# Two steps moved out of a feed-forward's first stage, and two squares summed by TensorE: one edit to a two-network kernel on one core

## The reference, cut to what matters

```python
for l in range(2):
    h = h + 0.5 * swiglu(rmsnorm_2(h, ffn1_norm[l]), ...)      # ffn1_0, ffn1_1
    u = rmsnorm_2(h, mix_norm[l])
    if l == 0:
        h = h + pool_mixer(u, pool_w[0], pool_scale[0])        # the pooling
    else:
        h = h + mla_attention(u, ..., k_nope, k_rope, v, cos, sin)
    h = h + 0.5 * swiglu(rmsnorm_2(h, ffn2_norm[l]), ...)      # ffn2_0, ffn2_1
    if l == 0:                                                  # mla_shared_kv
        ckr = rmsnorm_2(h, kv_in_norm) @ w_dkv
        c_kv = rmsnorm_2(ckr[..., :256], kv_latent_norm)        # latent norm
        k_rope = apply_rope(ckr[..., 256:], cos, sin)           # key rotation
        k_nope, v = c_kv @ w_uk, c_kv @ w_uv
out = rmsnorm_2(h, final_norm)[:, 16:]
```

## Time and profile before

| what | value |
|---|---|
| median of 3 runs | 1303.61 us (1303.28, 1303.61, 1309.53) |
| the profiled execution | 1307.76 us, its span 1306.4 us |
| mean granted TensorE clock | 0.976 |
| PE busy | 1248.9 us, 96% of the span |
| DVE busy | 898.9 us, 69% |
| ACT busy | 632.9 us, 48% |
| POOL busy | 182.7 us, 14% |

### The profile page before, as it was taken

The page is one execution under the profiler, slowest core; times in us unless marked ns, Lnnn a source line. Parts: engine busy times, 40 slices in busy tenths (PEclk is TensorE's granted clock), DMA queues, the critical chain, the costliest instruction groups (busy, mean ns, idle before and its releaser), DMA issues.

```text
span 1306.4 us, 23696 instructions
## 1 busy us (share of the span) xinstructions
PE 1248.9 (96%) x9876; PEld 1211.8 (93%) x9876; DVE 898.9 (69%) x1283; ACT 632.9 (48%) x973; POOL 182.7 (14%) x181
## 2 busy tenths in 40 slices
PE   4999999999999999998899999989999999999996
PEld 3988899999999999998799999989999977999996
DVE  7969889877566766657866656776666564766653
ACT  4545545766444444434544444444454454654531
POOL 2005434000141000013200001300001311000022
PEclk7999999999999999998899999989999988999998
DMA  8956564667655555653255565455555621555540
GB/s 323 370 203 216 203 242 153 242 237 273 195 163 177 170 169 179 195 176 128 98 162 176 179 194 177 130 162 192 187 180 191 191 95 50 182 189 194 185 155 33
DMA packets 66994, 238.87 MB, mean 183 GB/s; under 512 B 7302, under 2 KB 9528, under 8 KB 66888
## 3 DMA queue, kind: packets, MB, share of 16 engines
q1 hardware_dynamic: 66296, 235.17, 53.6%
q0 software_dynamic: 592, 2.19, 0.5%
HBM read 236.26 MB, written 1.07 MB: 182 GB/s over the span
## 4 chain that ended last, share of the span: by engine, by line
PE 82%; DVE 12%; ACT 2%; issue 2%; DMA 2%; POOL 1%; SPq 0%; DVEq 0%; ACTq 0%
PE G L560 25%; PE G L561 25%; PE G L562 24%; DVE sb_wlo L1349 3%; DMA sb_raw<-in_wstream 2%; DVE sb_hidf L1436 1%; PE G L580 1%; DVE sb_rstd L1399 1%; PE A L694 1%; PE A L670 1%; ACT sb_whi L1013 0%; DVE sb_xl L1861 0%; PE A L580 0%; DVE sb_X L1724 0%; PE A L681 0%
## 5 line engine op out<-in xcount | busy, mean ns | idle before, releaser
L1349 DVE TENSOR_TENSOR sb_wlo<-sb_raw,sb_whi 128x1024 fp32r<-128x1024 f32 x395 | 487.7, 1267 | 93.2 <-ACT sb_whi L1013 93.0
L560 PE MATMUL G<-sb_xh,sb_whi 128*128 128x256 f32 (+2 forms) x1764 | 504.0, 286 | 13.3 <-DVE sb_gu L1649 7.5
L561 PE MATMUL G<-sb_xl,sb_whi 128*128 128x256 f32 (+2 forms) x1764 | 502.9, 285 | 0.0
L562 PE MATMUL G<-sb_xh,sb_wlo 128*128 128x256 f32 (+2 forms) x1764 | 501.6, 284 | 0.0
L1013 ACT ACTIVATE sb_whi<-sb_raw 128x1024 fp32r<-128x1024 f32 x395 | 404.6, 1050 | 195.1 <-PE G L562 166.2
L560 PEld LDWEIGHTS G<-sb_xh,sb_whi 128*128 128x128 f32 x1764 | 334.8, 190 | 17.5 <-DVE sb_gu L1649 8.4
L562 PEld LDWEIGHTS G<-sb_xh,sb_wlo 128*128 128x128 f32 x1764 | 334.6, 190 | 0.0
L561 PEld LDWEIGHTS G<-sb_xl,sb_whi 128*128 128x128 f32 x1764 | 334.4, 190 | 0.0
L560 PE MATMUL G<-sb_hh,sb_whi 128*128 128x256 f32 (+1 forms) x1056 | 298.8, 283 | 0.7 <-DVE sb_hh L1539 0.7
L562 PE MATMUL G<-sb_hh,sb_wlo 128*128 128x256 f32 (+1 forms) x1056 | 298.1, 282 | 0.0
L561 PE MATMUL G<-sb_hl,sb_whi 128*128 128x256 f32 (+1 forms) x992 | 280.3, 283 | 0.0
(11 more groups left out here) (302 smaller groups left out, 1316.5 us busy)
## 6 DMA issues: line engine op xcount, KB each, us to landing
sb_raw<-in_wstream SPq DMA_DIRECT2D x443, 512.0 KB, 4.4
sb_bias<-bias_scratch POOLq DMA_DIRECT2D x1, 2048.0 KB, 16.9
sb_X<-in_xT SPq DMA_DIRECT2D x2, 512.0 KB, 7.0
out_T<-sb_X SPq DMA_DIRECT2D x4, 256.0 KB, 2.2
sb_con<-in_consts SPq DMA_DIRECT2D x1, 632.0 KB, 6.7
sb_vec<-in_vecs SPq DMA_DIRECT2D x1, 82.5 KB, 1.9
sb_X<-in_metaT POOLq DMA_DIRECT2D x1, 64.0 KB, 4.7
sb_boh<-in_bias_oh SPq DMA_DIRECT2D x1, 51.0 KB
```

The source lines that it names most:

```text
L560: e.matmul(out, w_h, xs, start=k0 + s.kt == 0, stop=False)
L561: e.matmul(out, w_h, xr, start=False, stop=False)
L562: m = e.matmul(out, w_l, xs, start=False, stop=k0 + s.kt == ktotal - 1)
L1349: e.tensor_tensor(wlo[:, i % NSPLIT, 0:w], raw[:, c % NRAW, 0:w], f(whi[:, i % NSPLIT, 0:w]), ALU.subtract).then_inc(lo_done, 1)
```

## The change

- `mean` adds up to three matmuls in one PSUM group for the stages in `APART` ("ffn1_0", read at the pooling, and "ffn2_1", read at the output): `sumsq`, then the two buffers of `sq`. POOL's `squares_of` leaves out the two additions of the last two squares there. The counts of `sumsq_done` are set to match. ACT waits at the pooling for the mean instead of for the squares before it writes over `sq`.
- The key rotation moves on DVE from behind `krope` to behind `down0`'s low parts of the third feed-forward.
- The latent norm moves on ACT and DVE from the middle of `gu01` to behind `down1`'s part. PE's mean for it stays where it was.
- POOL's mask rows wait until DVE has made the low part of the third feed-forward's hidden tile 3.

```diff
+APART = ("ffn1_0", "ffn2_1")
...
-        SUMSQ = {n: 15 * (k + 1) for k, n in enumerate(("wout", "mlp_out", "ffn1_0", "ffn2_0"))}
+        SUMSQ = {"wout": 15, "mlp_out": 30, "ffn1_0": 43, "ffn2_0": 58}
...
-        SUMSQ["ffn2_1"] = SUMSQ["wo"] + 15
+        SUMSQ["ffn2_1"] = SUMSQ["wo"] + 13
...
             def mean(which, cols, stage, bank=0, of=None):
...
-                e.matmul(A[bank][:, 0:n], mean_ones[:, which, :], (of or sumsq)[:, cols], start=True, stop=True).then_inc(mean_done, 1)
+                parts = [(of or sumsq)[:, cols]] + ([sq[:, k, cols] for k in range(2)] if stage in APART else [])
+                for k, part in enumerate(parts):
+                    m = e.matmul(A[bank][:, 0:n], mean_ones[:, which, :], part, start=k == 0, stop=k == len(parts) - 1)
+                m.then_inc(mean_done, 1)
...
-            e.wait_ge(sumsq_done, SUMSQ["ffn1_0"])
+            e.wait_ge(mean_done, MEAN["mix0"])
...
-            swiglu("ffn1_1", latent_factor, lambda i: x_hi("ffn1_1_down", i, COLS1, lambda kt: V("mix_norm1", kt)))
+            def mix1_high(i):
+                x_hi("ffn1_1_down", i, COLS1, lambda kt: V("mix_norm1", kt))
+                if i == 1:
+                    latent_factor()
+            swiglu("ffn1_1", lambda: None, mix1_high)
...
-            e.wait_ge(con_in, 16)
...
-            e.tensor_copy(khead[HD:QK, :, :], krot[:, :].unsqueeze(1).broadcast_to([ROPE, MH, T])).then_inc(khead_rope, 1)
+
+            def key_rotation():
+                e.wait_ge(con_in, 16)
...
+                e.tensor_copy(khead[HD:QK, :, :], krot[:, :].unsqueeze(1).broadcast_to([ROPE, MH, T])).then_inc(khead_rope, 1)
...
-            swiglu("ffn1_1", latent_factor, RSTD["kv"], lambda i: x_lo("mix1", i, COLS1, lambda kt: V("mix_norm1", kt)))
+            def mix1_low(i):
+                x_lo("mix1", i, COLS1, lambda kt: V("mix_norm1", kt))
+                if i == 0:
+                    key_rotation()
+                if i == 1:
+                    latent_factor()
+            swiglu("ffn1_1", lambda: None, RSTD["kv"], mix1_low)
...
             def squares_of(name, cols, used, after=None):
...
+                apart = name[:-5] in APART
                 e.wait_ge(mean_done, MEAN[used])
                 for kt in range(KT):
                     e.wait_ge(left_dve, plan.left_dve[f"{name}{kt // 2}"] - 1 + kt % 2)
-                    square(X[:, kt, cols], kt == 0, cols)
+                    if apart and kt == KT - 2:
+                        e.wait_ge(sumsq_done, squares[0])
+                    square(X[:, kt, cols], kt == 0, cols, not apart or kt < KT - 2)
...
             e.wait_ge(ckv_copied, 1)
+            e.wait_ge(hid_lo, HID["ffn1_1"] + 4)
             mask_rows(khead, "mla_k", T)
```

More of the change, by code:

```diff
@@ L1753, in vector_program @@
             e.tensor_tensor(tmp[0:64, 0, :], G[plan.pair["krope"]][0:64, 0, 0:T], rstd[0:64, :], ALU.mult).then_inc(left_dve, 1)
-            e.wait_ge(con_in, 16)
[L1755 to L1761, removed]
-            e.tensor_copy(khead[HD:QK, :, :], krot[:, :].unsqueeze(1).broadcast_to([ROPE, MH, T])).then_inc(khead_rope, 1)
+            def key_rotation():
+                e.wait_ge(con_in, 16)
+                e.wait_ge(left_dve, plan.left_dve["krope"])
+                e.tensor_tensor(krot[:, :], tmp[0:32, 0, :], cosT(0, 32, ALL), ALU.mult).then_inc(krope_step, 1)
+                e.wait_ge(krope_step, 1)
+                e.tensor_tensor(tmp[0:32, 1, :], tmp[32:64, 0, :], sinT(32, 64, ALL), ALU.mult).then_inc(krope_step, 1)
+                e.wait_ge(krope_step, 2)
+                e.tensor_tensor(krot[:, :], krot[:, :], tmp[0:32, 1, :], ALU.add).then_inc(krope_step, 1)
+                e.wait_ge(krope_step, 3)
+                e.tensor_copy(khead[HD:QK, :, :], krot[:, :].unsqueeze(1).broadcast_to([ROPE, MH, T])).then_inc(khead_rope, 1)
             def latent_factor():
@@ L1885, in pool_program, with square @@
             squares, turn = [0], [0]
-            def square(src, first, cols):
+            def square(src, first, cols, add=True):
                 if first:
@@ L1895, in square @@
                     squares[0] += 1
+                    if not add:
+                        return
                     e.wait_ge(sumsq_done, squares[0])
```

## The result

The changed kernel took 1297.13 us (median of 7 runs, 1293.46 to 1298.91), the kernel before 1304.93 beside it (median of 7, 1303.28 to 1309.71). The ratio is 0.9931, with a 95% interval of 0.991 to 0.9951. The forecast time was 1297.1 us, but the forecast difference was -6.5, and the medians differ by 7.8. The interval excludes 1: the gain of 0.7% is clear of the noise.

The account below looks back on a forecast made before the run. PE is busy 96% of the span, so gains lie only in its waits, low clock or tail. -4.08 - 2.3 + 0.1 + 0.4 - 0.65 = -6.5 us from 1303.61 gives 1297.1 us, range 1294.0 to 1301.2.

Parts of the forecast that it names:

- The wait at the start: Third feed-forward: PE's wait before `gu3` falls from 4.38 to 0.68 us and a 0.38 wait goes: -4.08 us.
- The clock: Third feed-forward behind `gu3`: with 0.68 us of wait left TensorE's clock doesn't fall: -2.3 us, bounds 0 and 2.3.
- rival A: Third feed-forward's `gu3`: 1.88 us of wait remains and the clock falls behind it: 1300.6 us, chance 0.12.
- Where the pieces land: Third feed-forward's down products: rotation behind `down0` costs 0, latent norm behind `down1` is just in time: +0.1 us.
- rival B: `down2`: latent norm beside POOL takes up to 2.2 us longer, PE waits 1 to 2 us: 1299.5 us, chance 0.13.
- The start, clock and landing together: Third feed-forward: the terms for wait, clock and moved pieces together, -6.28 us.
- The pooling: At the pooling two more fp32 products make the mean's result 0.43 us later: +0.4 us, bounds 0 and 0.92.
- The output: At the output the mean starts 1.52 us earlier, less 0.86 for two more products: -0.65 us.
- The sum: Whole kernel: all terms make -6.5 us, set against the median 1303.61: 1297.1 us; chance 0.66.

Follow-up runs that it names:

- x4: Kernel before with only the latent norm and the mask rows moved; rotation and means as before: 1297.42 us, ratio 0.9931.
- x3: Kernel before with only the key rotation and the mask rows moved; latent norm and means as before: 1302.45 us, ratio 0.9971.
- x7: Kernel before with nine unread filler products ahead of the third feed-forward's `gu3`, in PE's wait: 1301.82 us, ratio 0.9977.
- x8: Changed kernel with the key rotation moved behind `down1` too, beside the latent norm: 1300.79 us, ratio 0.9974 to the kernel before.
- x1: Changed kernel with both means built as before, so only rotation, latent norm and mask rows moved: 1297.81 us, ratio 0.9937 to the kernel before.
- x9: Changed kernel with the pooling's mean ahead of the last mixing product and three unread fillers before `ffn2_0`'s `gu3`: 1294.58 us, ratio 0.9924 to the kernel before.
- x2: Kernel before with only the two TensorE means added; rotation, latent norm and mask rows not moved: 1304.46 us, ratio 0.9991.
- x6: Changed kernel with the pooling's mean one product earlier, ahead of the last mixing product: 1296.49 us, ratio 0.9937 to the kernel before.

## Why the prediction was right, and where it was off

- **The wait at the start.** 4.38 became 0.68 and the 0.38 before it went, as forecast. Its price was a little low: 4.08 was the sum of the recorded waits, but `gu3` starts 4.39 us earlier, counted from the `kv` reciprocal (25.32 in the three traces of before, 20.93 and 20.97 in the two of the changed kernel). The 0.38 costs 0.68 from start to start. The reason was right in that DVE's pieces ahead make the wait, and incomplete in taking them as one: without the latent norm there is no wait, whether the rotation stands there or not (x4), and beside the latent norm rotation and mask rows make 2.38 of it (x3). That the mask rows' copy held up DVE there isn't in the prediction.
- **The clock.** Forecast -2.3; by x7 2.19 to 2.52. It stayed at 1.00 behind 0.68 us, and rival A (1.88 us left, the clock lost) didn't come about.
- **Where the pieces land.** Forecast +0.1 at a margin of zero; PE has no wait in the down products. In the trace DVE's pieces took from 999.87 to 1004.45, the same 4.58 us as before, and x8 measures the margin: 0.05 us, or 0.27 by the recorded wait. The contention with POOL that was to decide rival B wasn't there: POOL's addition took 0.74 us from 1000.50 and lay wholly beside the reciprocal. The Trainium skill, GPSIMD Engine Reference, Specifications, which would spare a reciprocal, agrees with that.
- **The start, clock and landing together** were forecast as -6.28. Means over the traces give 208.29 - 214.99 = -6.7. The first trace had the smallest of the three stretches before. With 4.37 for the start, 2.3 are left for the clock.
- **The pooling.** Forecast +0.43, measured +0.31 to +0.36; the reciprocal is later although two additions went, as said.
- **The output.** Forecast -0.65, measured -0.71 to -0.77. PE's wait for POOL and its two added products stand in the rows (changed kernel, in order of time):

```profile
1285.91 1.18 POOL L1910 TENSOR_TENSOR sb_sq<-sb_X 128x256 f32<-128x256 f32 x2 [10.73 <-DVE sb_X L1415]
1287.24 0.67 PE L591 MATMUL A<-sb_sumsq,sb_mean_ones 128*128 128x256 f32 x2 [1.87 <-POOL sb_sq L1910]
1287.75 1.03 PE L591 MATMUL A<-sb_sq,sb_mean_ones 128*128 128x256 f32 x4
```

- **The sum.** The terms measured in the stretches make -6.7 + 0.34 - 0.74 = -7.1 against -6.5. The whole difference is larger. Over the three sets the kernel before has a mean of 1305.13 us (59 runs), the changed one, with its first 7 runs, 1297.03 (15 runs): -8.1, with a standard error of 0.8. So the sum was too small by 0.6 to 1.6 us, and it was set against a median of three runs (1303.61) that lay 1.1 us under the median of 59 (1304.70). That the forecast time met the median to 0.1 us is luck: the two errors cancelled.

What stays open is the 1.0 us between -7.1 and -8.1. It lies little beyond the standard error. From each run's mean clock, 2 x (1 - clock) x span gives the time at half clock: 48.9 us before, 36.3 changed. Of the 12.6 us less the third feed-forward accounts for 6.8 in the traces (862.3 to 869.1 in the first). The tail from about the output's reciprocal on, where PE has no matmul left, accounts for some 3.5 (7.6 us at half clock before, 4.1 changed, means of their traces), and that costs nothing: from the reciprocal to the end it is 7.3 us in all 14 traces. Whether the other 2.3 are chance, or whether a kernel that loses its clock once meets its later waits at a worse moment, these runs don't tell. Reckoned the same way (mean gain less the gain in the three stretches), x1 and x4 to x9, which keep the clock at the third feed-forward's `gu3`, have 1.0, 1.8, 0.2, 0.0, 1.4, 2.0 and 2.2 us over; x2 and x3, whose clock still falls there, have -0.1 and 0.0. With 5 to 12 runs of each that is a hint at the second and doesn't show it.

## What to carry to other kernels

When several pieces stand ahead of a wait, their durations don't say which one makes it. Look at where the engine would stand idle without each, and move one at a time: here one move gave the whole 4.39 us, the other 2.38 without it and nothing behind it. An instruction of another engine that goes away with them is a piece too (POOL's mask rows). Before a gain in one trace is credited to a change, cut both traces at common marks and see whether it lies where the change acts; take a second trace of each kernel. And when an addition goes to TensorE, place the product where its input is ready: moving one line brought 1.5 us where the added products had cost 0.35.

## What the runs showed of the hardware

- A half clock can cost nothing. Between the pooling's reciprocal and `ffn2_0`'s the mean clock went from 0.78 to 0.89, and the stretch took 31.11 to 31.14 us in all 14. In x6, for one, DVE was busy for 28.7 of the 30 us from 606 to 636, and PE waited for it in between. In the third feed-forward 6.8 us at half clock, up to 2.0 of them still in the wait, cost 2.2 to 2.5.
- The same wait of 1.88 us at the second feed-forward's `gu3` had a half clock behind it in the first trace of before and none in the second and third. The Trainium skill, TensorE: Matmul & The Clock Gate, What's actually happening, says that the watch on activity runs on its own and isn't reset when the kernel starts. The traces agree: the same wait did and did not have the clock fall behind it.
- The clock goes with the spread of the kernel before: its 59 runs go from 1302.2 us at a mean clock of 0.982 to 1311.5 at 0.975, and all eight over 1308 are at 0.978 or less.
- PE's recorded idle time can understate what a wait costs: 0.38 us cost 0.68 from start to start, 3.35 (x8) cost 3.57.
- POOL held up DVE's instructions of two inputs and not one of one input: a low part took 2.91 us beside POOL's mask copy and the next 1.21 without it, while a reciprocal took 1.84 us beside POOL's addition and 1.84 before without one.
- A wait filled with products that nobody reads kept the clock (x7, one trace), at no cost in time, since the products ended before the data came.
